# A fused fp32 three-block network on one Trainium2 core: the gated linear attention's norm by 4-column sums, three norms shared with ScalarE, four transposition banks after the third norm, and one gate projection moved into the attention's first pair

## What is computed

```python
def rms_norm(x, g):
    xf = x.astype(jnp.float32)
    y = xf * lax.rsqrt(jnp.mean(xf * xf, axis=-1, keepdims=True) + RMS_EPS)
    return (y * g.astype(jnp.float32)).astype(x.dtype)
...
    o = rms_norm(o, gla_norm_g.reshape(GLA_HEADS, GLA_HV)) * jax.nn.silu(g).reshape(bn, sn, GLA_HEADS, GLA_HV)
    mix = jnp.concatenate([rg_out, o.reshape(bn, sn, GLA_VDIM)], axis=-1)
    return mix @ w_out
...
    q, k, v, g, fl = jnp.split(proj, [D_MODEL, 2 * D_MODEL, 3 * D_MODEL, 4 * D_MODEL], axis=-1)
...
    return (o * jax.nn.sigmoid(g)) @ w_out
```

## Time and profile before

| | us |
|---|---|
| median of 3 runs | 3862.73 (3862.09 to 3863.27) |
| the profiled execution | 3853.49 |
| its span, first to last instruction | 3851.8 |
| PE busy in it | 3671.5 (95%) |
| DVE, POOL, ACT busy | 1946.5, 1687.7, 1168.2 |

### The profile page before, as it was taken

One profiled execution on the slowest core, in us unless ns is written; L12 is line 12 of the kernel. 1 busy time (PEld: TensorE's weight loads), 2 busy tenths in 40 slices (PEclk: granted clock), 3 DMA queues, 4 the chain that ended last, 5 costly groups with the idle time before them and its releaser, 6 DMA issues.

```text
span 3851.8 us, 49830 instructions
## 1 busy us (share of the span) xinstructions
PE 3671.5 (95%) x18038; PEld 2976.8 (77%) x18038; DVE 1946.5 (51%) x3245; ACT 1168.2 (30%) x1888; POOL 1687.7 (44%) x1802
## 2 busy tenths in 40 slices
PE   6998999999999899999979999999997999999997
PEld 5777778888887667777758888888786778888886
DVE  6864563333344466665674222223599464444446
ACT  5422231111113555555533111111315232222222
POOL 2642267455551422322235654444563484444342
PEclk8999999999999999999989999999999999999999
DMA  6321013323320011111110211111111111111111
GB/s 229 123 72 33 23 44 98 99 87 93 96 84 23 23 45 44 40 44 50 34 44 29 65 51 53 44 44 44 38 56 44 55 44 49 49 44 54 43 55 44
DMA packets 248501, 224.57 MB, mean 58 GB/s; under 512 B 12661, under 2 KB 194579, under 8 KB 248356
## 3 DMA queue, kind: packets, MB, share of 16 engines
q1 hardware_dynamic: 222240, 171.09, 14.8%
q10 hardware_dynamic: 26115, 51.53, 4.2%
HBM read 218.33 MB, written 4.26 MB: 58 GB/s over the span
## 4 chain that ended last, share of the span: by engine, by line
PE 88%; DVE 7%; ACT 2%; POOL 1%; issue 1%; SPq 0%; DMA 0%; ACTq 0%; DVEq 0%; POOLq 0%
PE PS L718 12%; PE PS L719 12%; PE PS L720 12%; PE PS L851 6%; PE PS L853 6%; PE PS L852 6%; PE PS L1119 3%; PE PS L745 3%; PE PS L747 3%; PE PS L746 3%; PE PS L1120 3%; PE PS L1121 3%; PE PS L1165 2%; PE PS L1179 2%; PE PS L1198 2%; DVE PS L2828 1%
## 5 line engine op out<-in xcount | busy, mean ns | idle before, releaser
L718 PE MATMUL PS<-UH,WH 128*128 128x512 f32 (+1 forms) x2192 | 864.0, 394 | 17.0 <-POOL WL L3189 9.2
L3189 POOL TENSOR_TENSOR WL<-RAW,WH 128x256 fp32r<-128x256 f32 x1017 | 848.6, 865 | 21.3
L719 PE MATMUL PS<-UL,WH 128*128 128x512 f32 (+1 forms) x2192 | 857.3, 391 | 0.0
L720 PE MATMUL PS<-UH,WL 128*128 128x512 f32 (+1 forms) x2192 | 856.8, 391 | 0.0
L3186 POOL TENSOR_SCALAR WH<-RAW 128x1024 fp32r<-128x1024 f32 x255 | 276.7, 1085 | 1287.9 <-PE PS L720 457.5
L718 PEld LDWEIGHTS PS<-UH,WH 128*128 128x128 f32 (+1 forms) x2192 | 413.4, 189 | 109.1 <-issue 11.7
L2207 DVE TENSOR_TENSOR X<-PS,X 128x512 f32<-128x512 f32 x432 | 292.7, 687 | 401.8 <-PE PS L853 390.1
L720 PEld LDWEIGHTS PS<-UH,WL 128*128 128x128 f32 (+1 forms) x2192 | 412.6, 188 | 88.7
L719 PEld LDWEIGHTS PS<-UL,WH 128*128 128x128 f32 (+1 forms) x2192 | 413.2, 189 | 86.0 <-issue 0.2
L851 PE MATMUL PS<-WH,HH 128*128 128x512 f32 x1024 | 401.1, 392 | 0.0
L853 PE MATMUL PS<-WL,HH 128*128 128x512 f32 x1024 | 399.2, 390 | 0.0
(11 more groups left out here) (359 smaller groups left out, 5973.4 us busy)
## 6 DMA issues: line engine op xcount, KB each, us to landing
RAW<-in_mlp_w_dram SPq DMA_DIRECT2D x128, 512.0 KB, 4.1
ADM<-in_ada_w_dram ACTq DMA_DIRECT2D x96, 256.0 KB, 3.3
RAW<-in_w_up_dram SPq DMA_DIRECT2D x44, 512.0 KB, 3.9
ADR<-in_ada_w_dram ACTq DMA_DIRECT2D x32, 512.0 KB, 4.4
WR<-in_od_w_in_dram SPq DMA_DIRECT2D x32, 512.0 KB, 4.2
RAW<-in_w_down_dram SPq DMA_DIRECT2D x22, 512.0 KB, 3.3
RAW<-in_ev_w_in_dram SPq DMA_DIRECT2D x20, 512.0 KB, 4.0
RAW<-in_w_in_dram SPq DMA_DIRECT2D x20, 512.0 KB, 3.9
```

The lines of the kernel that those rows point to most:

```text
L718: pe.matmul(bank(b)[0:width], wh, xh, start=(k == 0), stop=False)
L719: pe.matmul(bank(b)[0:width], wh, xl, start=False, stop=False)
L720: mm = pe.matmul(bank(b)[0:width], wl, xh, start=False, stop=(k == NK - 1))
L3189: ins = pool.tensor_tensor(WL[slot][:, c], r[:, c], WH[slot][:, c].bitcast(F32), ALU.subtract)
```

## The change

1. **GLA norm.** `sums(u)` multiplies each 128x128 block of GSQ by one column of ones: four matmuls of 128x1, tokens now along partitions, so that a token half is 128x4. Root (ACT) and reciprocal (DVE) work on 128x4. `spread(u)` brings it back: four matmuls of 128x128 of the broadcast column with the identity, into bank 7, which DVE multiplies with OO straight from PSUM (`normed`). `mixed(0)` and `mixed(1)` go ahead of the last gate item; `sums(0)`, `sums(1)`, `spread(0)`, `spread(1)` sit inside it after blocks 0, 3, 6 and 7; `sums(3)`, `spread(2)`, `spread(3)` sit between the first output items. ACT and DVE get a matching order, and DVE's steps for u = 3 and the rest lie between the additions of the output rows. Root and silu are of different tables, and ACT now goes silu, root, silu, root in a pair.
2. **Shared norms.** At norms 1, 3 and 5 ACT makes tiles 2 and 3 of the first token half (`share_norm`), from one more 128x4 product of DVE; DVE makes tiles 0 and 1.
3. **Banks.** The 8 transpositions of the first half after norm 3 rotate over banks 6, 7, 2, 3 instead of 6, 7.
4. **Attention.** The gate projection of pair 0, token half 0, leaves the prologue and becomes step 4's item of pair 0 (blocks 0 to 3 before the scores, 4 to 7 after the values). Slots 2 and 3 of the later k and output tiles change places, and the rotation of banks 5, 6, 7 shifts by one.

```diff
 RESID_STEPS = (1, 3)
+SHARED_NORMS = (1, 3, 5)
+XH, XA = {}, {}
+for _n in range(1, 6):
+    for _t in range(8):
+        _to = XA if _n in SHARED_NORMS and _t in (2, 3) else XH
+        _to[_n, _t] = len(_to) + 1
...
-    if i in (2, 4) and p:
+    if i in (2, 4) and (p or i == 4):
         item = ("g", p, 1 if i == 2 else 0)
...
-    if _key[:2] == ("u", 0):
-        T_BANK.append((6, 7, 2, 3)[_i % 4])
+    if _key[:2] == ("u", 0) or _key[:3] == ("u", 3, 0):
+        T_BANK.append((6, 7, 2, 3)[_key[3] % 4])
...
-                    column("k", n, n * P + D, 2 + p % 2, ("k", n, 0))
+                    column("k", n, n * P + D, 3 - p % 2, ("k", n, 0))
...
-        GRS = at("GRS", [P, HALF], top + 2 * KB)
+        GLR = (RSUM, NMX)
...
                 mm.then_inc(done if signal is None else signal, 1)
-            def out_rows(rows, halves=(0, 1)):
+            def out_rows(rows, halves=(0, 1), between=None):
                 for h in halves:
...
+                    for i, (tb, mh) in enumerate(BY_BLOCK[h]):
                         c = slice(mh * HALF, (mh + 1) * HALF)
                         out_item(d_bank(), tb, mh, [(t[0][:, c], t[1][:, c], xh[:, half(h)], xl[:, half(h)])
                                                     for t, xh, xl in rows])
+                        if between is not None:
+                            between(i)
...
-                    def squares(u):
+                    def sums(u):
                         pe.wait_ge(S("gsq"), 4 * p + u + 1)
-                        if 4 * p + u >= 2:
-                            pe.wait_ge(S("gla_std"), 4 * p + u - 1)
-                        pe.matmul(bank(6 + u % 2), ONES[:, :], GSQ[:, :], start=True, stop=True)\
-                            .then_inc(S("gla_sum"), 1)
+                        if p:
+                            pe.wait_ge(S("gla_std"), 4)
+                        for t in range(4):
+                            mm = pe.matmul(bank(6)[:, 4 * u + t:4 * u + t + 1], GSQ[:, t * P:(t + 1) * P], ONES[:, 0:1],
+                                           start=True, stop=True, skip_group_check=True)
+                        mm.then_inc(S("gla_sum"), 1)
+
+                    def spread(u):
+                        pe.wait_ge(S("gla_inv"), 4 * p + u + 1)
+                        if 4 * p + u:
+                            pe.wait_ge(S("gla_o"), 4 * p + u)
+                        for t in range(4):
+                            v = GLR[p][:, 4 * u + t:4 * u + t + 1].broadcast_to([P, P])
+                            mm = pe.matmul(bank(7)[:, t * P:(t + 1) * P], v, IDENT[:, :],
+                                           start=True, stop=True, skip_group_check=True)
+                        mm.then_inc(S("gla_wide"), 1)
                     a_free.wait_at(NA)
                     d_free.wait_at(ND - 4)
@@ -1056,22 +1079,22 @@
                     states(6)
                     t = tile()
                     u_item(t, 0)
-                    u_item(t, 1)
                     pe.wait_ge(S("mod_ready"), 4)
                     d_free.wait_at(ND)
                     mixed(0)
                     mixed(1)
-                    squares(0)
+                    early = {0: lambda: sums(0), 3: lambda: sums(1), 6: lambda: spread(0), 7: lambda: spread(1)}
+                    u_item(t, 1, between=lambda k: early.get(k, lambda: None)())
                     mixed(2)
-                    squares(1)
                     mixed(3)
-                    squares(2)
-                    squares(3)
+                    sums(2)
                     out = [(tile(), GMH[hh], GML[hh]) for hh in range(2)]
                     pe.wait_ge(S("m_ready"), 4 + 4 * p + 2)
-                    out_rows(out, (0,))
+                    late = {0: lambda: sums(3), 2: lambda: spread(2), 3: lambda: spread(3)}
+                    out_rows(out, (0,), lambda i: late.get(i, lambda: None)())
                     if p == 1:
                         pe.wait_ge(S("gla_std"), 8)
+                        pe.wait_ge(S("gla_o"), 8)
                         t_gate(1)
                     pe.wait_ge(S("m_ready"), 4 + 4 * p + 4)
...
                 turn_v(("vt", 0, 0))
-                item(("g", 0, 0), every)
...
+            def share_norm(n):
+
+                act.wait_ge(S("nmr"), SHARED_NORMS.index(n) + 1)
+                for t in (2, 3):
+                    act.activation(X[:, t, :], X[:, t, :], ACT.Identity, bias=NMX[:, t:t + 1],
+                                   scale=RS[:, t:t + 1]).then_inc(S("xa"), 1)
...
                     act.wait_ge(S("qk_ready"), 3 * p + 3)
-                    for i in range(2):
-                        for h in range(2):
-                            free(act.activation(B[2 + i][:, half(h)], ev_bank(("g", p, i, h)), ACT.Silu))
+                    def silu(i, h):
+                        free(act.activation(B[2 + i][:, half(h)], ev_bank(("g", p, i, h)), ACT.Silu))
                     def copy_o(u):
                         free(act.activation(OO[u][:, :], ev_bank(("o", p, u)), ACT.Copy))
@@ -1704,33 +1732,38 @@
                     def root_o(u):
                         act.wait_ge(S("gla_sum"), 4 * p + u + 1)
-                        act.activation(GRS[:, :], bank(6 + u % 2), ACT.Sqrt, bias=EPSR[:, :], scale=1.0 / P)\
-                            .then_inc(S("gla_std"), 1)
+                        act.activation(GLR[p][:, 4 * u:4 * u + 4], bank(6)[:, 4 * u:4 * u + 4], ACT.Sqrt,
+                                       bias=EPSR[:, :], scale=1.0 / P).then_inc(S("gla_std"), 1)
                     def high_o(u):
                         go.take()
                         act.activation(GMH[u % 2][:, half(u // 2)], OO[u][:, :], ACT.Copy).then_inc(S("gmh"), 1)
+                    silu(0, 0)
+                    silu(0, 1)
+                    silu(1, 0)
                     copy_o(0)
                     square(0)
                     copy_o(1)
                     root_o(0)
                     square(1)
+                    root_o(1)
+                    silu(1, 1)
+                    high_o(0)
+                    high_o(1)
                     copy_o(2)
-                    high_o(0)
-                    root_o(1)
                     square(2)
                     copy_o(3)
-                    high_o(1)
                     root_o(2)
                     square(3)
+                    root_o(3)
                     high_o(2)
-                    root_o(3)
                     high_o(3)
                     if p == 1:
                         t_gate(1)
                 gd.skip(len(EV_ITEMS))
                 block_stds(0)
+                share_norm(1)
                 t_u(1, 0, *range(NK))
...
-            def xhat(h):
+            def xhat(n, h):
                 ns.take()
                 r = RS[:, 4 * h:4 * h + 4]
                 chain.done(dve.reciprocal(r, r))
+                if h == 0 and n in SHARED_NORMS:
+                    dve.scalar_tensor_tensor(out=NMX[:, 0:4], in0=MV8[:, 0:4, 0], scalar=-1.0, in1=r,
+                                             op0=ALU.mult, op1=ALU.mult).then_inc(S("nmr"), 1)
                 for t in range(4 * h, 4 * h + 4):
-                    x = X[:, t, :]
-                    dve.tensor_scalar(x, x, MV8[:, t, 0:1], RS[:, t:t + 1], ALU.subtract, ALU.mult)\
-                        .then_inc(S("xh"), 1)
+                    if (n, t) in XH:
+                        x = X[:, t, :]
+                        dve.tensor_scalar(x, x, MV8[:, t, 0:1], RS[:, t:t + 1], ALU.subtract, ALU.mult)\
+                            .then_inc(S("xh"), 1)
             def ul(n, h, *ks):
...
                                 mine.wait_at(0)
-                    for u in range(4):
+                    def gain(u):
                         hh, h = u % 2, u // 2
                         dve.wait_ge(S("gsq"), 4 * p + u + 1)
                         chain.done(dve.scalar_tensor_tensor(out=OO[u][:, :], in0=OO[u][:, :],
                                                             scalar=pv("ev_gla_norm_g", 2 * p + hh),
                                                             in1=B[2 + hh][:, half(h)], op0=ALU.mult, op1=ALU.mult))
+
+                    def inverse_o(u):
                         gst.take()
-                        chain.done(dve.reciprocal(GRS[:, :], GRS[:, :]))
-                        dve.tensor_tensor(OO[u][:, :], OO[u][:, :], GRS[:, :], ALU.mult).then_inc(S("gla_o"), 1)
+                        r = GLR[p][:, 4 * u:4 * u + 4]
+                        dve.reciprocal(r, r).then_inc(S("gla_inv"), 1)
+
+                    def normed(u):
+                        dve.wait_ge(S("gla_wide"), 4 * p + u + 1)
+                        dve.tensor_tensor(OO[u][:, :], bank(7), OO[u][:, :], ALU.mult).then_inc(S("gla_o"), 1)
+
+                    def low_o(u):
+                        hh, h = u % 2, u // 2
                         gmh.take()
```

(33 more changed lines are left out.)

38 lines of the change are left out of this document (22 added, 16 removed).

## The result

The changed kernel takes 3828.93 us (median of 4 runs, 3827.05 to 3831.5) against 3862.41 us (4 runs, 3858.32 to 3863.27): the ratio is 0.9916, 95% interval 0.9899 to 0.9933. With five more runs later its median over nine is 3831.5 (3827.05 to 3835.83), and 35 more of the kernel before lay between 3857.2 and 3863.3, the median of each group near 3860.5. The forecast was 3831.4 in a range of 3823 to 3844.

The account below looks back on a forecast made before the run. PE was taken to bound the kernel (88% of its chain). GLA norm 18.4, attention 5.9, norm 3 6.5 and norm 5 0.5 sum to 31.3 us off 3862.7, giving 3831.4, range 3823 to 3844.

Parts of the forecast that it names:

- GLA norm, 18.4: GLA tails: each falls from 56.8 to 47.6 us, gain 9.2 a pair, 18.4 for both.
- all output matmuls 0.39: Sign that the forecast is right: in the GLA tails every output matmul lasts 0.39 us, with no wait above 1 us.
- The slow rival: GLA tails: new waits drop PE's clock, all 240 matmuls slow adds 58 us, 3889; decides from some 163; chance 0.03.
- My upper end, 12.5 a pair: GLA tails: the most a pair could gain, if small groups take 0.42 us and nothing waits.
- Table loads: ACT's two added loads a pair cost 1.28 us each, without the skill's drain (about 2.66 for load and drain).
- Attention, 5.9: Attention's prologue and pair 0's step 4: 4.8 us off, 1.4 lost, 2.5 given back, net 5.9.
- Step 4's part: Attention, pair 0: gate item fills a 4.24 us hole, `turn_probs` 1.4 us late, 2.5 given back.
- The upper end, 6.5: Attention: the most it could gain, if the chain in step 4 isn't pushed at all.
- the other queues: I cost that at nothing: Attention: ACT's moved gate copy and POOL's and SP's tiles in exchanged slots cost nothing.
- Norm 3, 6.5: Norm 3 to first projection: sharing (2.1 us) and four banks together end that projection 6.5 us sooner.
- Norm 5, 0.5: Norm 5: PE's 0.53 us wait behind DVE's x-hats goes, gain 0.5.
- the difference should carry over unchanged: The profiled execution lies 9.2 us under the median; the forecast 31.3 was taken off the median 3862.7 all the same.

Follow-up runs that it names:

- b1: The kernel before, unedited, run again for a second profile; 3860.25 us.
- a1: The changed kernel, unedited, run again for a second profile; median 3833.27 us, ratio 0.993.
- x4: The changed kernel without the shared norms, DVE making all four tiles at norms 1, 3 and 5; median 3835.19 us.
- x10: The changed kernel with x9's and x5's edits together; median 3827.48 us, ratio 0.9918.
- x2: The changed kernel with part 4 undone: gate item back in the attention's prologue, with its slots; median 3833.84 us.
- x3: The changed kernel with two banks instead of four for the transpositions after norm 3; median 3829.31 us.
- x1: The changed kernel with the old GLA norm (128x512 roots and reciprocals, old order); median 3849.38 us.
- x9: The changed kernel with two up tiles of mlp 1 exchanging slots, not the tile intended, so POOL's three tiles stayed; median 3830.95 us.
- x11: The kernel before with part 4 alone (gate projection in step 4, slots swapped); median 3851.28 us, ratio 0.9977.
- x5: The changed kernel with DVE in mlp 1 making the second half's low parts UL ahead of the residual passes; median 3827.74 us.

## Why the prediction was right, and where it was not

**The total**: 31.3 forecast, 33.5 in the first comparison, 29.0 over nine runs. It came out by errors that cancel. Norm 3 gave nothing where 6.5 were forecast, and places for which nothing was forecast gave time instead: b1 and the change's first profile are 29.6 apart, and 5.6 of that lie in the attention's later pairs; b1 and a1 are 25.4 apart, 2.1 of it there. That the total came within 2.5 us of the forecast is in good part luck.

**GLA norm, 18.4**: the step held. The sum of one tail was 47.6; where no matmul was slow it took 47.7 (x4, x10). Groups cost 0.81 against my 0.85, `spread(1)` waited 0.18 against 0.3, `sums(3)` 0.3 against 0.8. The first output row stands 22.4 to 22.6 behind the tail's start instead of 27.3: 4.7 to 4.9 nearer, not 5.5. Not in the sum were the slow matmuls: 0, 6 or 12 in the first pair (47.7, 48.6, 50.2) and 0 to 18 in the second (49.4 to 53.6, with the gate transpositions), so the sign "all output matmuls 0.39" failed. Both tails together gained 11.6 (before's first profile against x2's and x3's tails) to 19.4 (its second against x4's), 16.1 to 17.9 by the medians of x1. The slow rival thus has a true core, a clock that falls in the tail, but with 30 slow matmuls at most where it needed 163. Its price was too high as well: 0.24 is what a slow matmul lasts longer, but its successor starts only 0.20 later, by which it needed 195. My upper end, 12.5 a pair, was a wrong sum: with groups at 0.42 and no wait my own terms give 56.8 − 43.1 = 13.7.

**Table loads**: 1.28, with the root 0.02 behind. The Trainium skill's figure ("ScalarE: Activation LUTs", "What ACT_TABLE_LOAD costs") of a drain on top of the load is not borne out by these rows.

**Attention, 5.9**: 6.1 to 7.0 in its own stages by the two profiles of each kernel, 4.4 with x9's. Step 4's part was right to a tenth: `turn_probs` 1.30 late against 1.4, and 2.1 to 2.6 given back behind it against 2.5, as the slow matmuls behind the hole are gone. The prologue's transpositions came the forecast 4.8 sooner; up to the first `turn_probs` it gave 3.2 (54.3 to 51.1) or 6.2 (57.3), by whether slow matmuls followed the wait of before. The upper end, 6.5, was a wrong sum too: without the 1.4 it is 7.3.

But **the step that said "the other queues: I cost that at nothing" failed.** The slot swap made the tile that is held to the end another one, and POOL's list behind the last row grew from two ungated tiles to three (x2 against the change and x11). Alone that costs nothing (x11: 27.0 for norm 3's second part, as before). Beside parts 2 and 3, which bring PE there sooner, it costs norm 3 4.1 to 5.9 (55.7 to 57.5 against x2's 51.6). That part 4 does it is shown; that it is the slot, and not the bank order, rests on the plan's code and POOL's order of work, and no run here separates them.

**Norm 3, 6.5**: the first half of the step is nearly right, the end of the first projection comes 5.2 us sooner (29.3 to 24.1 behind the last row), 6.7 where no up matmul is slow. Sharing was sized too high: the first transposition comes 1.6 sooner (10.66 to 9.08) and not 2.1, as DVE's new small product takes 0.54 where I took 0.2. What failed is that I ended the sum there: I asked what bounds the first projection and not what the earlier PE meets next. It meets DVE, which must make x-hats, high-low differences and residual passes in list order before the next UL, and POOL, whose passes run beside them. POOL's four WL pieces go from 2.77 to 6.09 and DVE's residual pass from 1.21 to 3.10 where both run. The Trainium skill ("SBUF — State Buffer", "SBUF: two separate sides") says that a GpSimd operation and a DVE operation in a 2-port mode, or one with two inputs in SBUF, exclude each other by a lock that the first holds to its end; the longer passes on both sides agree with that. The x-hats, which have one such input, are held up as well; whether they run in a 2-port mode no run here shows. Four of them take 2.98 where POOL is idle (at 1221.42, ahead of the attention) and 4.54 to 6.64 beside it at norm 3. One, started at 2012.61 inside a gate pass of POOL from 2012.10 to 2014.94, takes 2.88 instead of 0.81 and ends 0.55 behind that pass.

Undoing part 4 (x2, 4.1 to 5.9 off) or reordering DVE (x5 and x10, 3.4 to 6.5 off) shows the step's gain was there to be had: x2's 51.6 is 4.7 under before, x10's 51.0 is 5.3. Undoing the banks (x3) removes the wait but gives up the 3.9 that they had won.

**Norm 5, 0.5**: right, 0.8 by the traces (x4 above). **Norm 1, nothing**: from tail 1's end to the first forget-gate matmul it is 767.6 to 768.7 in all fourteen profiles, with sharing or without. **Profile against median**: "the difference should carry over unchanged" was wrong in its ground. The first profiled execution was the fastest of some forty of that kernel; the medians' difference is what carried over.

## What to carry to other kernels

A stage that gets earlier must be followed until the next place where PE waits again, with the in-order lists of the other engines laid beside it; that is where four banks (3.9 us) and shared norms (1.6) won time and handed it to a wait 24 us later. A list that grows on another engine may cost nothing as long as PE comes late, and several us once PE comes sooner, as POOL's third tile probably did. An edit of weight slots is an edit of the order in which another phase's tiles can be prepared: count what stands behind the last use. And undo parts within the changed kernel as well as alone: part 4 is worth 9.1 alone and 0.6 to 2.3 inside, the last not clear of the spread. Where two profiles of one kernel differ by as much as the effect, compare the waits and the count of slow matmuls, not the stage's length.
